# One low-part subtraction per weight slot, or two of half the width, in a streaming encoder step

## The reference: what is computed

```
xn = rms_norm(x, norm_mix_w)
h, gb, gc, q, k, v, g_conv, g_attn = split(xn @ w_in)
y_c = gb * causal_conv3(gc * h)
y_a = window attention of q, k, v with sinks (chunks of 64, window 128)
x = x + (sigmoid(g_conv) * y_c + sigmoid(g_attn) * y_a) @ w_out
xn = rms_norm(x, norm_ffn_w)
x = x + (silu(xn @ w_gate) * (xn @ w_up)) @ w_down        # 1024 -> 2816 -> 1024
```

## Time and profile before

| | |
|---|---|
| median of 3 runs | 1702.38 us (1702.34 to 1702.88) |
| the profiled execution's own time | 1701.26 us |
| its span | 1699.5 us |
| TensorE busy | 1673.3 us, 98% |
| VectorE busy | 956.2 us, 56% |
| ScalarE busy | 693.3 us, 41% |
| GpSimd busy | 886.0 us, 52% |
| low parts of slots on GpSimd (L674) | 396 instructions |

### The profile page before, as it was taken

One profiled execution on the slowest core, in us unless ns is written; L12 is line 12 of the kernel. 1 busy time (PEld: TensorE's weight loads), 2 busy tenths in 40 slices (PEclk: granted clock), 3 DMA queues, 4 the chain that ended last, 5 costly groups with the idle time before them and its releaser, 6 DMA issues.

```text
span 1699.5 us, 27837 instructions
## 1 busy us (share of the span) xinstructions
PE 1673.3 (98%) x10510; PEld 1567.4 (92%) x10510; DVE 956.2 (56%) x1520; ACT 693.3 (41%) x1567; POOL 886.0 (52%) x808
## 2 busy tenths in 40 slices
PE   7999999999999999999999999999999999999999
PEld 7999888899889999999888899999989999999998
DVE  5466664636564412322568666757777555655555
ACT  6333566636665111111116444454454334333331
POOL 3544443333431212111239887887889656666662
PEclk9999999999999999999999999999999999999999
DMA  5211111111110111114120333233232322222222
GB/s 176 47 38 37 47 33 35 41 30 45 33 32 26 50 38 38 50 37 161 39 87 26 100 100 121 79 100 125 94 124 88 102 91 74 75 75 80 95 75 87
DMA packets 136056, 120.29 MB, mean 71 GB/s; under 512 B 24194, under 2 KB 117662, under 8 KB 135936
## 3 DMA queue, kind: packets, MB, share of 16 engines
q1 hardware_dynamic: 130400, 115.89, 21.8%
q10 hardware_dynamic: 4896, 2.36, 0.5%
q0 software_dynamic: 640, 0.43, 0.1%
HBM read 113.33 MB, written 5.32 MB: 70 GB/s over the span
## 4 chain that ended last, share of the span: by engine, by line
PE 94%; DVE 2%; POOL 1%; issue 1%; DMA 1%; ACT 1%; SPq 0%; DVEq 0%; POOLq 0%; ACTq 0%
PE banks L1503 37%; PE banks L1789 28%; PE banks L1850 15%; PE banks L1728 5%; PE banks L1666 2%; PE banks L1648 2%; PE banks L1526 1%; PE banks L1628 1%; PE banks L1539 1%; POOL xc_lo L681 1%; PE banks L1637 0%; DMA X<-in_x_prompt 0%; DVE xc_full L1331 0%; PE banks L1671 0%; PE banks L1516 0%
## 5 line engine op out<-in xcount | busy, mean ns | idle before, releaser
L1503 PE MATMUL banks<-x_hi,w_hi 128*128 128x384 f32 x1200 | 410.7, 342 | 0.0
L1503 PE MATMUL banks<-x_hi,w_lo 128*128 128x384 f32 x1200 | 401.8, 335 | 0.0
L1503 PE MATMUL banks<-x_lo,w_hi 128*128 128x384 f32 x1200 | 401.6, 335 | 0.0
L1789 PE MATMUL banks<-xc_hi,ring_a 128*128 128x256 f32 (+1 forms) x1200 | 249.2, 298 | 3.9 <-DVE u L1398 3.9
L1503 PEld LDWEIGHTS banks<-x_hi,w_hi 128*128 128x128 f32 x1200 | 225.4, 188 | 4.4
L1503 PEld LDWEIGHTS banks<-x_lo,w_hi 128*128 128x128 f32 x1200 | 225.6, 188 | 0.0
L1503 PEld LDWEIGHTS banks<-x_hi,w_lo 128*128 128x128 f32 x1200 | 225.3, 188 | 0.0
L507 POOL TENSOR_TENSOR w_lo<-w_raw,w_hi 128x1024 fp32r<-128x1024 f32 x31 | 81.6, 2632 | 272.5 <-ACT w_hi L720 272.5
L1789 PEld LDWEIGHTS banks<-xc_hi,ring_a 128*128 128x128 f32 x1200 | 197.7, 191 | 4.5 <-DVE u L1398 4.1
L674 POOL TENSOR_TENSOR ring_a<-raw_f,ring_a 128x512 fp32r<-128x512 f32 x133 | 189.8, 1440 | 19.7 <-ACT ring_a L948 18.7
L515 POOL TENSOR_TENSOR w_lo<-w_raw,w_hi 128x256 fp32r<-128x256 f32 x84 | 60.6, 752 | 228.2 <-ACT w_hi L720 228.2
(11 more groups left out here) (229 smaller groups left out, 3409.6 us busy)
## 6 DMA issues: line engine op xcount, KB each, us to landing
w_raw<-in_w_in SPq DMA_DIRECT2D x104, 256.0 KB, 3.1
raw_f<-in_w_gate SPq DMA_DIRECT2D x88, 256.0 KB, 3.7
raw_f<-in_w_up SPq DMA_DIRECT2D x88, 256.0 KB, 3.6
raw_f<-in_w_down SPq DMA_DIRECT2D x88, 256.0 KB, 3.5
X<-in_x_prompt SPq DMA_DIRECT2D x16, 512.0 KB, 8.9
w_raw<-in_w_out SPq DMA_DIRECT2D x16, 256.0 KB, 3.1
out_y_prompt<-X SPq DMA_DIRECT2D x16, 256.0 KB, 2.0
X<-in_x_sample SPq DMA_DIRECT2D x2, 512.0 KB, 11.8
```

The lines of the kernel that those rows point to most:

```text
L1503: mm = pe.matmul(banks[:, bank, 0:G], ws[slot][w][:, kt * P:(kt + 1) * P], xs[x][:, kt, g * G:(g + 1) * G], start=(kt == 0 and n == 0), st ...
L1789: mm = pe.matmul(banks[:, bank, 0:nb], ring(n)[:, w, k * P:(k + 1) * P], xc[x][:, X_OF_PROD[j], k, 0:nb], start=(start and k == 0 and z == 0),
```

## The change

The single subtraction of a slot is issued as two, the first over columns 0 to 255 and the second over 256 to 511. In a down slot these are plain column ranges; in a gate or up slot, which is seen as 4 blocks of 128 columns, they are blocks 0 and 1, then 2 and 3. Only the second signals `f_lo`. Nothing else changes: no buffer, no wait, no order.

```
     def slot_lo(n):
         gp.wait_ge(f_hi, n + 1)
-        gp.tensor_tensor(slot_view(n, 1), slot_source(n), slot_view(n, 0).bitcast(F32), ALU.subtract).then_inc(f_lo, 1)
+        flat = UNIT[SLOT_OF[n][0]][2] == 2
+        for half in range(2):
+            part = (slice(None), slice(256 * half, 256 * half + 256)) if flat else \
+                (slice(None), slice(2 * half, 2 * half + 2), slice(None))
+            ins = gp.tensor_tensor(slot_view(n, 1)[part], slot_source(n)[part], slot_view(n, 0)[part].bitcast(F32),
+                                   ALU.subtract)
+        ins.then_inc(f_lo, 1)
```

## The result

The changed kernel takes 1716.68 us (median of 6 runs, 1714.49 to 1720.78) against 1702.36 us (6 runs, 1701.26 to 1702.88) of the kernel before beside it: a ratio of 1.0087 [1.0077, 1.0097], or 14.3 us slower. The prediction of no measurable change was wrong, and its range ended at 1704.4 us.

A forecast was written before the change was run, and what follows sets the result against it. TensorE was taken to bound both bodies, with GpSimd's added time hidden there. -0.6 at the first stall and -0.8 between the passes gave -1.4 us, from 1702.38 to 1701.0 us; 8-in-10 range 1698.6 to 1704.4.

The forecast's parts named there:

- rival 2: Body of pass 0: GpSimd becomes the bound, 31.9 us a chunk against TensorE's 31.1; 1708 us, chance 0.05.
- the 792 instructions and their 740 ns: Sign in the profile after: GpSimd's subtraction line appears 792 times, with a median near 740 ns.
- the stall on L1398: Sign at the start of pass 0: TensorE's 3.9 us wait for VectorE shrinks to near 3.3 us.
- The second sum in mid pass 0: Sign in mid pass 0: VectorE's L1323 takes nearer 1.15 than 1.66 us.
- The load's cover: Body of pass 0: raw weights still land in time for VectorE's sums, 1.5 us of margin against 0.9 of lateness.
- Rival 3: Body of pass 0: late raw weights push sums by up to 0.5 us in 9 chunks; 1705.5 us, chance 0.07.
- the body: Bodies of both passes: none of GpSimd's added 51 us is on the path, so 0 if the covers hold.
- they take turns: VectorE and GpSimd on SBUF inputs: a sum beside busy GpSimd falls from 1.71 to 1.15 us, four sums 1.3 less.
- The first stall: At 940 us: slots 0.7 us later, the sum group 1.3 us shorter, so L1398 comes 0.6 us earlier.
- Between the passes: Sums make VectorE 1.6 us earlier, TensorE's waits for GpSimd eat 1.0 of 1.7 us of stalls; 0.8 gained.

The follow-up runs named there:

- Resting whole slots: The kernel before, whole slots, with GpSimd waiting for its own last slot at each slot: 1709.49 us, ratio 1.0040.
- the split by unit: Two kernels with a GpSimd wait every fourth slot: halves in gate and down slots only, 1703.73 us; halves in up slots only, 1704.84 us.
- either remedy: The changed kernel with a GpSimd wait every fourth slot, 1712.12 us; or with the first half of each unit's raw weights loaded earlier, 1710.85 us.
- the probe: A separate program: VectorE adds two SBUF tiles behind k back-to-back GpSimd subtractions; at 256 columns 0.93 us at k = 14, 8.41 us at 16.
- both remedies: The changed kernel with the first half of raw weights loaded earlier and a GpSimd wait every fourth slot: 1708.05 us, ratio 1.0032.
- the early load alone: The changed kernel with the first half of each unit's raw weights loaded earlier, without added GpSimd waits: 1710.85 us, ratio 1.0047.

## Why the prediction was wrong

**Right.** Two halves cost 1.38 us in place of 1.25, and a two-input sum beside a busy GpSimd about 1.15 in place of 1.71. GpSimd did not become the bound of pass 0 (rival 2). Of the signs named ahead, the 792 instructions and their 740 ns came true. GpSimd was busier by 75 us, not 45 to 60, the stall on L1398 grew to 4.6 us instead of shrinking to 3.3, and TensorE was not without a gap. The second sum in mid pass 0 came to 1.105 us as I had said, but I had compared it with 1.66, and there it had taken 0.69.

Two steps failed, and the runs price them apart in the body of pass 0: the cover of the load (3.1 us) and the taking of turns (4.9 us).

**"The load's cover: 1.5 us of margin against 7 x 0.13 = 0.9 us of lateness. It holds."** The lateness was 2.3 us. I counted only the seven slots of the up unit and let them start on time, since ScalarE had set their start. But the 1.37 us of idle time ahead of the first one was a reserve, not a guarantee. The gate unit's halves used it up, the start moved by 1.6 us, and VectorE waited 1.07 us for the load. Resting whole slots and the split by unit show it. Rival 3 named this mechanism, with a chance of 0.07 and 0.5 us a chunk; it came in four chunks of nine, with 0.7 to 0.8 us each. I priced the body at 0, and it lost 7.9.

**"Each sum waits out one whole GpSimd instruction", and "they take turns".** True behind a short run of GpSimd instructions, false behind a long one. The rows I read had runs broken by other VectorE work, and none of the kernel before was long enough. Six shut-outs of 3.5 to 8.8 us came of it, three of them in the body. The Trainium skill, "SBUF — State Buffer", section "Who interferes with whom", says of VectorE's modes that use both ports that whoever issues first gets the pair for the whole instruction. The trace agrees as far as one instruction goes. At 1121.95 us GpSimd got its access again for seven more; the rule is silent on who wins the next one, and I filled the gap with "they take turns".

**The first stall, -0.6.** It was longer, 4.6 us in place of 3.9. The group of four sums began 0.2 us late, within my term, but its first one was shut out:

```profile
933.19 4.79 DVE L1327 TENSOR_TENSOR w_sums<-raw_f 128x512 f32<-128x512 f32 x1 [0.74 <-DMA raw_f<-in_w_gate]
938.01 0.69 DVE L1329 TENSOR_TENSOR w_sums<-w_sums,raw_f 128x512 f32<-128x512 f32 x1
938.62 0.69 DVE L1330 TENSOR_TENSOR raw_f<-raw_f 128x512 f32<-128x512 f32 x1
```

The three behind it took 0.6 us each, since GpSimd had run dry, so the group needed 6.6 us, 5.9 before.

**Between the passes, -0.8.** Lost 5.0. I read only the two stalls at its end; the chain of waits of the changed kernel shows where it was decided:

```profile
1258.14 0.38 SPq L452
...
1259.59 4.38 DMA raw_f<-in_w_gate
1263.99 0.70 DVE w_sums L1327
```

The gate weights of pass 1 are asked for 0.7 us behind the border and the sums start 6.5 us behind it; before, that was 2.6 us ahead and 3.8 behind. The sums stand in VectorE's order ahead of the mixing (L1337) and the norm (L1089), for which TensorE then waits, and the border's 24 matmuls on ring_o behind that wait took 7.34 us against 5.72, with a granted clock of 0.70 from 1275 to 1280 us, a mean of the full 2.4 GHz and of 1.2, where it was 1.00 before. Some 2.2 of the 5.0 us are idle time of TensorE (3.1 us against 0.9) and 2.8 are the slower matmuls and transposes behind it. Which share of the 5.5 us in the next chunk is due to each cause I can't part; its two shut-outs (4.5 and 8.8 us) and one late transfer (1.67 us) stand in it, and with either remedy both shut-outs and the loss were gone.

**What stays open.** What decides that VectorE is shut out: in the probe the step lies between 14 and 16 instructions, in the kernels both outcomes occur behind 10 to 15. Why the granted clock fell between the passes in the changed kernel and with both remedies, and not with the early load alone. And what a rest every fourth slot costs with whole slots.

## What to carry to other kernels

Before work is added to an engine that is "only" 82% busy, follow its idle gaps one by one to what is queued behind them: a gap set by another engine's signal is a reserve that several small delays share, and it must be charged with all of them, from the last point at which the engine was on time. Splitting GpSimd's instructions shortens each wait of VectorE on their shared access, but raises the count of an unbroken run; where that count can reach ten while VectorE has an operation with two SBUF inputs, look in the trace for one such operation that lasts as long as GpSimd's run, and break the run with a wait, if there are 0.12 us to spare for it. In the chain of waits it shows as "issue", not as a wait.

## What the runs showed of the hardware

- In the probe a VectorE operation with two SBUF inputs that arrives behind 16 or 20 unbroken GpSimd instructions is held to the end of the run: 5.18, 8.41 and 14.89 us at 128, 256 and 512 columns with 12 instructions queued; at 14 or fewer it waits for one (0.66, 0.93, 1.47 us). At 1024 columns 14 are enough, for 27.81 us. In the kernels it happened behind 10 halves, and did not happen behind 11 halves or 15 quarters.
- GpSimd's wait on its own semaphore every fourth instruction brought the same add down to 0.43 us; one wait costs GpSimd 0.12 us (a slot of 1.25 us became 1.37, one of 1.39 became 1.51).
- A GpSimd subtraction of two fp32 tiles costs 0.42, 0.69 and 1.25 us at 128, 256 and 512 columns, some 0.14 us of it for the instruction itself (an estimate from twice 0.69 less 1.25 and twice 0.42 less 0.69).
